# Hybrid attention block with fp32r weight splitting on one core: six places for split weights, the memory branch moved into the job loop, and a reordered first gate-up block

## The reference

```python
h = rms_norm(x, pre_mix_g)
(q_n, k_c, v_c, k_s, v_s, k_w, v_w, g_n, q_m, k_m, v_m, q_x,
 gate_nsa, gate_moba, gate_mem) = split_columns(h @ w_in)
...
y_nsa  = merge_heads(o_nsa) @ w_nsa_o      # 8 heads: compressed + selected + window
y_moba = merge_heads(o_m)   @ w_moba_o     # 4 heads
y_mem  = merge_heads(o_x)   @ w_mem_o      # 4 heads over 256 memory tokens
merged = (sigmoid(gate_nsa) * y_nsa + sigmoid(gate_moba) * y_moba
          + sigmoid(gate_mem) * y_mem)
x = x + rms_norm(merged @ w_mix_out, post_mix_g)
h = rms_norm(x, pre_ffn_g)
f = (silu(h @ w_ffn_gate) * (h @ w_ffn_up)) @ w_ffn_down
x = x + rms_norm(f, post_ffn_g)
```

## Time and profile before

| what | value |
|---|---|
| median of 3 runs | 420.07 us (419.51 to 420.63) |
| the profiled execution, its own time | 419.44 us |
| its span in the trace | 417.6 us, 1.8 us less than its time |
| PE busy | 408.4 us of the span (98%) |
| DVE, ACT, POOL busy | 260.5, 233.5, 40.2 us |
| DMA | 78.82 MB, mean 189 GB/s |
| granted PE clock | mean 0.998 of full |

### The profile page before, as it was taken

How to read it: one execution, slowest core, us unless ns; L and a number is a source line. 1 busy time by engine, 2 the same in 40 slices (tenths; PEclk the granted TensorE clock), 3 DMA queues, 4 the chain that set the end, 5 groups by cost and what they waited for, 6 DMA issues and landing times.

```text
span 417.6 us, 5875 instructions
## 1 busy us (share of the span) xinstructions
PE 408.4 (98%) x2070; PEld 328.3 (79%) x2070; DVE 260.5 (62%) x450; ACT 233.5 (56%) x402; POOL 40.2 (10%) x76
## 2 busy tenths in 40 slices
PE   8999999999999999999999999999999999999994
PEld 4787889877777777877787788888888888888883
DVE  4854965875776786649859665556555655545434
ACT  5654964577767766744646774544554454545321
POOL 3210020021212122126000000000000000000000
PEclk9999999999999999999999999999999999999999
DMA  8999993535344335366555467556655556666002
GB/s 294 393 335 369 375 334 111 194 112 191 112 152 141 100 104 199 102 239 215 193 173 165 138 227 227 169 176 196 201 178 169 174 185 198 202 202 193 9 0 100
DMA packets 52016, 78.82 MB, mean 189 GB/s; under 512 B 2076, under 2 KB 28488, under 8 KB 51992
## 3 DMA queue, kind: packets, MB, share of 16 engines
q1 hardware_dynamic: 50216, 73.52, 53.7%
q0 software_dynamic: 1344, 4.43, 3.2%
q10 hardware_dynamic: 432, 0.56, 0.4%
HBM read 77.43 MB, written 1.07 MB: 188 GB/s over the span
## 4 chain that ended last, share of the span: by engine, by line
PE 92%; DVE 2%; ACT 2%; DMA 1%; issue 1%; ACTq 0%; DVEq 0%
PE acc L1120 27%; PE acc L1122 26%; PE acc L1121 26%; PE ob L1361 3%; PE sbank L1310 3%; PE ptb L1324 2%; DMA gx<-in_gx 1%; PE ptb L1439 1%; PE acc L1159 1%; PE sbank L1231 1%; PE acc L1163 1%; DVE gates L951 1%; PE acc L1164 1%; DVE xl L796 1%; ACT xh L507 0%
## 5 line engine op out<-in xcount | busy, mean ns | idle before, releaser
L761 DVE TENSOR_TENSOR wl<-raw,wh 128x1024 fp32r<-128x1024 f32 (+1 forms) x126 | 152.7, 1218 | 92.9 <-ACT wh L474 92.4
L474 ACT ACTIVATE wh<-raw 128x1024 fp32r<-128x1024 f32 (+1 forms) x126 | 131.0, 1046 | 92.6 <-PE acc L1122 80.5
L1120 PE MATMUL acc<-wh,xh 128*128 128x512 f32 (+1 forms) x368 | 146.3, 398 | 1.1 <-DVE xl L796 1.1
L1122 PE MATMUL acc<-wh,xl 128*128 128x512 f32 (+1 forms) x368 | 142.2, 386 | 0.0
L1121 PE MATMUL acc<-wl,xh 128*128 128x512 f32 (+1 forms) x368 | 142.0, 386 | 0.0
L1120 PEld LDWEIGHTS acc<-wh,xh 128*128 128x128 f32 x368 | 69.1, 188 | 18.0 <-issue 4.9
L1122 PEld LDWEIGHTS acc<-wh,xl 128*128 128x128 f32 x368 | 69.1, 188 | 14.3
L1121 PEld LDWEIGHTS acc<-wl,xh 128*128 128x128 f32 x368 | 69.2, 188 | 12.5
L1120 PE MATMUL acc<-wh,ah 128*128 128x512 f32 x88 | 34.3, 390 | 0.0
L1122 PE MATMUL acc<-wh,al 128*128 128x512 f32 x88 | 34.3, 389 | 0.0
L1121 PE MATMUL acc<-wl,ah 128*128 128x512 f32 x88 | 34.2, 389 | 0.0
(11 more groups left out here) (187 smaller groups left out, 407.0 us busy)
## 6 DMA issues: line engine op xcount, KB each, us to landing
raw<-in_w_in SPq DMA_DIRECT2D x18, 1024.0 KB
raw<-in_w_ffn_gate SPq DMA_DIRECT2D x22, 512.0 KB
raw<-in_w_ffn_up SPq DMA_DIRECT2D x22, 512.0 KB
raw<-in_w_ffn_down SPq DMA_DIRECT2D x22, 512.0 KB
raw<-in_w_mix_out SPq DMA_DIRECT2D x4, 1024.0 KB
raw<-in_w_mem_kv SPq DMA_DIRECT2D x2, 1024.0 KB
raw<-in_w_nsa_o SPq DMA_DIRECT2D x2, 1024.0 KB
raw<-in_w_in SPq DMA_DIRECT2D x3, 512.0 KB, 7.2
```

Source lines behind the costliest of these rows:

```text
L474: nc.scalar.activation(wh[:, k, :, 0:w], raw[:, slot, 2 * half:2 * half + 2, 0:w], ACT.Copy).then_inc(hi_done, 1)
L761: nc.vector.tensor_tensor(wl[:, k, :, 0:w], raw[:, slot, 2 * half:2 * half + 2, 0:w], wh[:, k, :, 0:w].bitcast(F32), ALU.subtract).then_in ...
L1120: nc.tensor.matmul(bank[:, 0:w], h[:, k, c], wh[:, slot, s, 0:w], start=first, stop=False)
L1122: return nc.tensor.matmul(bank[:, 0:w], l[:, k, c], wh[:, slot, s, 0:w], start=False, stop=last)
```

## The change

Six places instead of four for split parts of the mixer's weights (`SUBS = 6`, hence `AHEAD = 5`); in the feed-forward it goes back to four (`FFN_SUBS`) from the thirteenth part on (`ring`, `last_user`). The text of the input projections' `evac_cols` is not touched, and its `v_last + AHEAD` grows by two; numbers written out, as in `hi_to(11)`, stay. `tmp` shares its room with the buffers behind it. The memory branch's projection moves into iterations 18 and 19 of the job loop, its `merge` into DVE's iterations 19 and 20, and the addition of memory to MoBA from POOL to DVE, iterations 21 and 22 (`add_memory`). The NSA gates' columns take the places behind (iterations 20 to 25 and two parts behind the loop). In the first gate-up block products with the high part of x stand ahead of those with the low part, and the two turns for t = 1 stand elsewhere in it. DVE makes the norm and the first residual of t = 1, and the low part of one more weight part, ahead of the low part of the second x bank.

```diff
-RAW, SUBS = 4, 4
-AHEAD = SUBS - 1
+RAW, SUBS, FFN_SUBS, IN_PIECES = 4, 6, 4, 4
+AHEAD, FFN_AHEAD = SUBS - 1, FFN_SUBS - 1
...
+FFN_PARTS = [[V_GU + 9, V_GU + 10, V_GU + 11, V_GU + 12], [V_GU + 13, V_GU + 14]]
...
+def ring(v):
+
+    w = v - V_GU
+    return w % SUBS if w < 2 * SUBS else w % FFN_SUBS
+
+
+def last_user(v):
+
+    return v - SUBS if v - V_GU < 2 * SUBS + FFN_SUBS else v - FFN_SUBS
...
-            for n in range(2):
-                for t in range(TILES):
-                    pool.wait_ge(ev[t], B_MEM + n + 1)
-                    c = slice(SLICE * n, SLICE * n + SLICE)
-                    moba, mem = gates[:, t, D:2 * D], gates[:, t, 2 * D:3 * D]
-                    nc.gpsimd.tensor_tensor(moba[:, c], moba[:, c], mem[:, c], ALU.add).then_inc(m_done, 1)
...
-                if n in (21, 25):
-                    evac_gate(B_GATE_MEM + (n - 21) // 4, V_GATE + n)
-
+                if n == 23:
+                    evac_gate(B_GATE_NSA, V_GATE + n)
+
+            hi_to(V_NSA - 1 + AHEAD)
+            evac_gate(B_GATE_NSA + 1, V_NSA - 1)
             hi_to(V_NSA + 2 + AHEAD)
...
-                if n in (17, 18):
+                if 17 <= n <= 20:
                     merge(B_MOBA + n - 17)
+                if n in (21, 22):
+                    add_memory(n - 21)
                 lo_to(V_GATE + n + look_ahead(n))
...
-            merge(B_MEM)
-            merge(B_MEM + 1)
             merge(B_NSA)
...
             gain(0, 1, 1, B_MIX)
-            round_lo(3, 1)
             norm(1, 4, 2, 4)
             add_residual(0, 1, 0, 2, x1_done)
-            lo_to(V_GU + 3)
+            lo_to(V_GU + 5)
+            round_lo(3, 1)
             add_residual(0, 1, 1, 2, x1_done)
...
-                if n in (16, 17):
-                    pe.wait_ge(ol_done, 1)
-                    whole_block(B_MOBA + n - 16, V_GATE + n, 1, oh, ol, 0)
+                if 16 <= n < 20:
+                    branch = (n - 16) // 2
+                    pe.wait_ge(ol_done, branch + 1)
+                    whole_block(B_MOBA + n - 16, V_GATE + n, 1, oh, ol, 2 * branch)
...
-            by_tiles(B_GU, V_GU, 4, xh, xl, 0, ready=4, after={(0, 2): [lambda: new_x_bank(1, 0)], (0, 3): [lambda: new_x_bank(1, 1)]})
+
+            def first_ffn_block():
...
+                for i in range(2):
+                    high(0, i)
+                for i in range(2):
+                    low(0, i)
+                high(0, 2)
+                new_x_bank(1, 0)
+                high(0, 3)
+                low(0, 2)
+                low(0, 3)
+                for half in range(2):
+                    for i in (2 * half, 2 * half + 1):
+                        high(1, i)
+                    if half == 0:
+                        new_x_bank(1, 1)
+                    for i in (2 * half, 2 * half + 1):
+                        low(1, i)
```

More of the change, by code:

```diff
@@ L212, in build_layer @@
             yb = sb("yb", [P, TILES, D], F32, late)
-            tmp = sb("tmp", [P, TILES, SLICE], F32, late)
+            with ExitStack() as early:
+                tmp = sb("tmp", [P, TILES, SLICE], F32, early)
             silu = sb("silu", [P, TILES, GU_W], F32, late)
@@ L716, in ffn_ah, with ffn_act @@
                 nc.scalar.activation(ah[:, bass.ds(i * 2, 2), :], ptb[:], ACT.Copy).then_inc(ah_done, 1)
-            def ffn_act(i, j, first):
+            def ffn_act(i, j, first, parts=None):
                 for s in range(4):
-                    if not first:
+                    if parts is None:
                         ffn_hi(i, j, s)
+                    elif s < len(parts):
+                        hi_to(parts[s])
                     if s == 2 and not first:
@@ L1080, in ffn_al, with ffn_dve @@
                                         ah[:, bass.ds(i * 2, 2), :].bitcast(F32), ALU.subtract).then_inc(al_done, 1)
[L1082 removed]
+            def ffn_dve(i, j, first, parts=None):
                 for s in range(4):
[L1084 removed]
+                    if parts is None:
                         ffn_lo(i, j, s)
+                    elif s < len(parts):
+                        lo_to(parts[s])
                     if s == 2 and not first:
```

158 lines of the change are left out of this document (92 added, 66 removed).

## The result

The changed kernel takes **430.53 us** (median of 4 runs, 430.43 to 431.2), the kernel before 420.12 us on the same chip (median of 4, 419.51 to 420.63). The ratio is 1.0262, with a 95% interval of 1.0249 to 1.0274.

What follows compares the result with a forecast made beforehand. The prediction took PE's stream of products, busy 98% of the span, plus its few gaps as the bound. Terms 10.3 + 2.4 + 0.3 - 0.6 - 0.1 = +12.3 us on 419.44 gave 431.7, median 432.4 us, range 428.5 to 435.5.

Steps and rivals of the forecast that it cites:

- The first turn of keys: Input projections: block 1 is taken out only after unit 6's load, PE's turn 10.3 us later; bounds 9.5 and 11.
- The clock: Behind that gap PE restarts at 1.2 GHz for some 5.4 us, losing 44%: +2.4 us, bounds 0 and 3.2.
- The job loop: Iterations 19 to 22: DVE gets 5.3 us more work and falls behind briefly: +0.3 us, bounds 0 and +2.5.
- The additions off POOL: Around the turns of `yb`: DVE freed of POOL's sharing, first wait goes, second stays 0.35: -0.6 us, bounds 0 and -0.9.
- The first gate-up block: High parts first remove waits of 0.68 and 0.44, new ones come: net -0.1 us, bounds -1.1 and +0.5.
- The sum: Whole kernel: the five terms add to +12.3 us, 431.7 us for the profiled execution.
- From the sum to the median: Whole kernel: the median lies 0.63 us above the profiled execution, so 431.7 becomes 432.4 us.
- The first (unit 6 in time): ACT's wait for part 12: load in by 30.3 us, no gap opens, about 419.7 us; chance 0.05.
- The second (the clock stays up, 430.0): Behind the gap: the clock stays up or comes back at once, sum +9.9, 430.0 us; chance 0.15.
- The third (DVE as the bound of iterations 19 to 24): Job loop: DVE becomes the bound, +2.5 in place of +0.3, 434.6 us; chance 0.12.
- What would show it: New timeline: among other signs, POOL 8 us less, and an `xl` wait of 0.5 to 1 us in the first gate-up block.

Runs made afterwards that it cites:

- experiment 1: Changed kernel, but ACT and DVE take blocks out behind v_last + 3 as before the change: 419.05 us, ratio 0.9978 to the kernel before.
- experiment 2: Kernel before the change with one wait added, ACT takes block 1 out only when unit 6 is loaded: 429.68 us, ratio 1.0227.
- experiment 3: Changed kernel plus 12 unused PE products of 512 columns ahead of the first turn of keys: 428.96 us.
- experiment 5: Changed kernel, block 1 alone taken out behind v_last + 3, other blocks keep v_last + 5: 423.07 us, ratio 1.007 to the kernel before.
- experiment 9: experiment 1 with four places for split parts all through: 418.83 us, ratio 0.9987; its profiled execution took 423.45 us.
- experiment 7: experiment 1 with the four memory additions back on POOL, inside job loop iterations 21 and 22: 419.58 us, ratio 0.9986.
- experiment 8: Kernel before the change with POOL's four additions on DVE, memory branch still behind the job loop: 420.06 us, ratio 1.0007.
- experiment 10: Kernel before the change, block 1 taken out behind part 9 (v_last + 2), ahead of unit 5's load: 419.5 us, ratio 0.9987.
- experiment 4: Changed kernel, block 1 alone taken out behind part 11 (second half of unit 5) instead of part 12: 422.24 us, ratio 1.0061.

## Why the prediction was right, point by point

- **The first turn of keys.** Forecast +10.3 us at 42.95, measured +10.2 at 42.88. Every link is in the rows: the load in at 39.80 (forecast 39.81), DVE's low part at 40.89 (40.90), its taking out at 42.03 (42.1), the turn 0.85 us behind (0.84). Experiments 1 and 2 show from both sides that this place is the cause. It could be computed that exactly because the load of unit 6 and ACT's wait for it were already in the trace of before: the change only moved a step from one side of that wait to the other.
- **The clock.** The term was right in kind and is the one that was mis-sized most: 2.4 us forecast, 1.8 measured by the shift of the events, 1.6 by the medians of experiment 3. The step that was off is "I take the value of the start, the nearest row": there the slow stretch had lasted 5.4 us, here 3.8. The rate of loss was right: products that follow each other by 0.43 us instead of 0.23 lose 47%, and 0.47 times 3.8 is 1.8. The lengths seen in these runs after a restart are 3.3 us (experiment 5), 3.8 (the change), 5.8 (experiment 2) and 5.9 (experiment 9), so one row had been too few for a point value; in experiment 2 the loss behind the gap was 2.6 us, above the forecast's 2.4. The bounds 0 to 3.2 held all four. The Trainium skill (TensorE: Matmul & The Clock Gate, Part 1) counts the ramp as under 1% of a span, and this trace agrees: 1.8 us are 0.4%.
- **The job loop.** Forecast +0.3, measured 0.0. The merges do fill DVE: it is busy for 15.37 us of the 16 from 168 to 184. But PE does not wait once in it. The forecast let DVE fall behind by 1.5 us and counted that as a touch for PE; it was within the slack of the turn of probabilities.
- **The additions off POOL.** Forecast -0.6, measured -0.8. The first wait at `yb` is gone, the second is 0.3, where 0.35 was forecast. The first figure is PE's whole gap: 1.06 us between two starts instead of 0.23. But the path to it was in part wrong. The forecast reads one low part that POOL holds up by 0.6 us and takes that for what DVE gains; the trace has two more such instructions (1.94 us at 186.99, 1.07 at 194.13), 1.7 us in all. And experiments 7 and 8 show that leaving POOL is not what closes the gap: with the additions on POOL within the loop the gain is the same, with them on DVE behind the loop there is none. It is closed by DVE having less to do in that stretch. That the sum came out near is partly luck: any change that lets DVE finish there 0.8 us sooner would close the whole gap, and none could win more.
- **The first gate-up block.** Forecast -0.1, measured 0.1 later (21.41 us before, 21.47 after, from the first turn of the new x to the first of `act_tok`). The wait for the last x bank was 0.3, the upper end of the forecast's 0.1 to 0.3. The one for the second low part was 0.4 and not 0.9: DVE had it at 240.9, which is 0.4 sooner than the forecast's 230.2 moved by 11.1, and PE came to it 0.2 later. And one was overlooked: "its table and norm work starts where it did: 0" fails, PE waits for `act_tok` for 0.5 us behind the block.
- **The sum.** 10.3 + 2.4 + 0.3 - 0.6 - 0.1 = 12.3 forecast, 10.2 + 1.8 + 0.0 - 0.8 + 0.0 = 11.2 by the events of the table, as by the two profiled executions (the 0.1 of the gate-up block stands against 0.1 less between the two turns of `yb`).
- **From the sum to the median.** The 0.63 us between the profiled execution of before and its median were carried over to the forecast. They should not have been. By experiment 10 they are most likely the scatter of unit 5's landing, and in the changed kernel the turn hangs on unit 6 instead: its runs lie at 430.43, 430.44, 430.63 and 431.2, its profiled execution 0.1 above the median. Of the 1.9 us by which the forecast is high, 0.6 are the clock, 0.5 the other terms and the remaining 0.8 this.
- **The rivals.** The first (unit 6 in time) fell by the ACT row at 39.80. The second (the clock stays up, 430.0) has the nearest number, but the wrong mechanism: the granted clock is 0.50 over 10 us. The third (DVE as the bound of iterations 19 to 24) fell with the 0.0 above.
- **The signs.** Two of those named in "What would show it" came out a little off: POOL has 7.5 us less and not 8, and the wait for `xl` is 0.4 us, below the 0.5 to 1 that was given.

## What to carry to other kernels

An engine works its list in order, so a step that another engine waits for (here: emptying a bank) must not stand behind a step that waits for a load which comes later than the bank is wanted. Look in the trace for idle time of that engine ended by a load, and ask on which side of it each release stands: a constant that raises how far ahead splits run moves releases across such waits, and every block has its own (block 1 behind unit 6, block 2 behind unit 8, the second hidden until the first is mended). More places for split weights are worth only the waits for splits that PE has; they can be had without moving the releases, by a second constant. And a load that lands near the point where it is wanted (unit 5 landed between 28.5 and 31.8 us in these traces, and only the earliest left PE hardly a wait) showed up as scatter of the runs and not in the median. Last, take what a gap costs from the start times of the products and not from the listed idle time alone.

## What the runs showed of the hardware

The granted clock did not fall at one fixed distance from the last product. In the change's 11.1 us gap it fell 4.7 us after PE's last product, and at the program's end 3.7 us after it; but in experiment 9 it fell 1.95 us after it, within a gap of 2.88 us, and in experiment 5 at the end of one of 3.00 us. Gaps of 1.82 and 1.97 us (experiment 4) left it up. So a stall of 3 us cost here 4.6 to 5.6 us in all (the stall, and 47% of a slow stretch of 3.3 or 5.9 us: an estimate), and that second cost is not proportional to the first: after the gap of 2.88 us the slow stretch lasted 5.9 us, after the one of 8.90 us (experiment 2) 5.8, after the one of 11.1 us 3.8. What sets these lengths stays open.

DVE and POOL do hold each other up, but each way. In experiment 7, DVE:

```profile
174.07 1.21 DVE L778 TENSOR_TENSOR wl<-raw,wh 128x1024 fp32r<-128x1024 f32 x1
175.21 0.17 DVE L1010 RECIPROCAL jst<-jst 128x2 f32<-128x2 f32 x1
175.41 1.05 DVE L1011 TENSOR_TENSOR jst<-jst,gsig 128x2 f32<-128x2 f32 x1
```

and POOL:

```profile
167.96 2.53 POOL L462 TENSOR_TENSOR gates<-gates 128x512 f32<-128x512 f32 x2
172.83 3.61 POOL L462 TENSOR_TENSOR gates<-gates 128x512 f32<-128x512 f32 x2
```

A product of two numbers per partition that takes 0.16 us elsewhere took 1.05 and ended at 176.46, when POOL's pair ended (176.44); and the pair took 3.61 us beside DVE's low part, 1.1 more than the pair before it. That is what the Trainium skill (SBUF — State Buffer, Who interferes with whom) says, that the loser waits for the winner's whole instruction. The forecast read the 1.83 us of a low part in the earlier trace rows as only 0.6 of contention and so as milder than that rule. The trace of before settles it: of POOL's four additions the third ran when that low part began at 191.66; it had begun at 190.05, took 2.36 us and ended at 192.41; the low part ended at 193.49, 1.08 us later. That fits a low part that waited for all that was left of POOL's addition, 0.75 us, of which 0.6 shows as added length. In all these rows the wait lies inside the instruction's own duration and not in the idle time before it.
